# The last two down units of a two-FFN encoder layer made for 192 tokens first and then for 128, with the final norm, transposes and stores of the first part placed among the products of the second

## The reference, cut to what matters

```python
x = x + 0.5 * _swiglu(_rmsnorm(x, ffn2_norm[l]), ffn2_w_gate[l], ffn2_w_up[l], ffn2_w_down[l])
...
y = _rmsnorm(x, final_norm)

def _swiglu(x, w_gate, w_up, w_down):
    return (jax.nn.silu(x @ w_gate) * (x @ w_up)) @ w_down
```

## Time and profile before

| | |
|---|---|
| median of three runs | 2367.65 us |
| the profiled execution | 2367.89 us |
| span of its records | 2365.6 us |
| TensorE busy | 2355.6 us, 100% of the span |
| VectorE busy | 1187.0 us, 50% |
| ScalarE busy | 809.0 us, 34% |
| DMA | 347.01 MB, mean 147 GB/s |

### The profile page before, as it was taken

How to read it: one execution, slowest core, us unless ns; L and a number is a source line. 1 busy time by engine, 2 the same in 40 slices (tenths; PEclk the granted TensorE clock), 3 DMA queues, 4 the chain that set the end, 5 groups by cost and what they waited for, 6 DMA issues and landing times.

```text
span 2365.6 us, 36473 instructions
## 1 busy us (share of the span) xinstructions
PE 2355.6 (100%) x16063; PEld 2333.1 (99%) x16063; DVE 1187.0 (50%) x945; ACT 809.0 (34%) x719; POOL 123.3 (5%) x64
## 2 busy tenths in 40 slices
PE   9999999999999999999999999999999999999998
PEld 9999999999999999999999899999999999999998
DVE  5444444444444445666695456434444444443445
ACT  5323223232232324353543444233232232323324
POOL 1000000000000000100100001000000000000000
PEclk9999999999999999999999999999999999999999
DMA  7444444444444444535345134444444444444442
GB/s 251 149 148 154 142 157 144 147 155 142 156 146 148 154 143 149 189 112 178 103 139 165 55 127 160 143 151 151 143 158 142 150 151 143 158 142 152 150 143 79
DMA packets 194617, 347.01 MB, mean 147 GB/s; under 512 B 10810, under 2 KB 35904, under 8 KB 194560
## 3 DMA queue, kind: packets, MB, share of 16 engines
q1 hardware_dynamic: 190864, 337.34, 43.8%
q0 software_dynamic: 2480, 7.63, 1.0%
q10 hardware_dynamic: 1216, 1.20, 0.2%
HBM read 340.50 MB, written 5.65 MB: 146 GB/s over the span
## 4 chain that ended last, share of the span: by engine, by line
PE 99%; DVE 1%; issue 0%; ACT 0%; POOL 0%; ACTq 0%; DVEq 0%; POOLq 0%
PE ps L1613 31%; PE ps L1614 31%; PE ps L1615 31%; PE ps L2005 0%; PE ps L2025 0%; PE ps L1732 0%; PE ps L2165 0%; PE ps L1993 0%; PE ps L1728 0%; PE ps L1849 0%; PE ps L1843 0%; PE ps L1822 0%; PE ps L2006 0%; PE ps L1789 0%; PE ps L1891 0%; DVE work L1352 0%
## 5 line engine op out<-in xcount | busy, mean ns | idle before, releaser
L1613 PE MATMUL ps<-mov_hi,w_hi 128*128 128x320 f32 x3568 | 1107.1, 310 | 0.4 <-DVE w_lo L1251 0.4
L1615 PE MATMUL ps<-mov_hi,w_lo 128*128 128x320 f32 x3568 | 1102.5, 309 | 0.0
L1614 PE MATMUL ps<-mov_lo,w_hi 128*128 128x320 f32 x3568 | 1102.5, 309 | 0.0
L1043 DVE TENSOR_TENSOR w_lo<-raw,w_hi 128x2048 fp32r<-128x2048 f32 x309 | 708.2, 2292 | 740.7 <-ACT w_hi L601 740.2
L601 ACT CAST w_hi<-raw 128x2048 fp32r<-128x2048 f32 x309 | 588.5, 1905 | 1418.3 <-PE ps L1615 1418.2
L1613 PEld LDWEIGHTS ps<-mov_hi,w_hi 128*128 128x128 f32 x3568 | 669.8, 188 | 1.9 <-issue 0.7
L1614 PEld LDWEIGHTS ps<-mov_lo,w_hi 128*128 128x128 f32 x3568 | 669.8, 188 | 0.6
L1615 PEld LDWEIGHTS ps<-mov_hi,w_lo 128*128 128x128 f32 x3568 | 669.7, 188 | 0.0
L1613 PE MATMUL ps<-h_hi,w_hi 128*128 128x320 f32 x1472 | 454.7, 309 | 0.0
L1615 PE MATMUL ps<-h_hi,w_lo 128*128 128x320 f32 x1472 | 454.4, 309 | 0.0
L1614 PE MATMUL ps<-h_lo,w_hi 128*128 128x320 f32 x1472 | 454.4, 309 | 0.0
(11 more groups left out here) (257 smaller groups left out, 768.7 us busy)
## 6 DMA issues: line engine op xcount, KB each, us to landing
raw<-in_ffn_w_up SPq DMA_DIRECT2D x88, 1024.0 KB, 5.1
raw<-in_ffn_w_down SPq DMA_DIRECT2D x88, 1024.0 KB, 5.0
raw<-in_ffn_w_gate SPq DMA_DIRECT2D x87, 1024.0 KB, 5.1
raw<-in_w_in SPq DMA_DIRECT2D x28, 1024.0 KB, 5.4
raw<-in_w_out SPq DMA_DIRECT2D x16, 1024.0 KB, 5.1
raw<-in_mla_w_uq SPq DMA_DIRECT2D x12, 256.0 KB, 4.2
raw<-in_w_in SPq DMA_DIRECT2D x4, 640.0 KB, 4.3
work<-in_x_prompt SPq DMA_DIRECT2D x8, 256.0 KB, 7.7
```

Of the source, the lines that this page charges most:

```text
L1043: dve.tensor_tensor(w_lo[:, n % SPLIT_SLOTS, :], raw[:, n % RAW_SLOTS, :], w_hi[:, n % SPLIT_SLOTS, :].bitcast(F32), ALU.subtract).then_in ...
L1613: pe.matmul(out, w[0], x[0], start=first, stop=False)
L1614: pe.matmul(out, w[0], x[1], start=False, stop=False)
L1615: return pe.matmul(out, w[1], x[0], start=False, stop=last)
```

## The change

The last two down units (`q` = 2 and 3) are no longer made by `unit` for 320 tokens. A new function `part` makes a unit for a range of tokens. The order on TensorE becomes: unit 2 for tokens 128 to 319 (`EARLY`), unit 3 for the same, unit 2 for tokens 0 to 127 (`LATE`), unit 3 for those. Each part is again 48 products with 48 weight loads. The squares, folds and gains of the last two chunks are split in the same way; the token sums of the early tokens, and jobs 0, 1 and 2, are put at fixed places among the 48 products of the last part (`between`). `Y_JOBS` now has the jobs of the early token tiles first (j0 t1, j0 t2, j1 t1, j1 t2, j2 t1, j2 t2, j3 t1, j3 t2) and then the four of token tile 0. The factors are made in two steps, `spread(1, ...)` for the early tokens and `spread(2, ...)` for the late ones. The steps that ScalarE and VectorE took after `ffn` are moved into their `tail_steps`, among the drains and squares. The queues of the stores are as before (jobs 0 to 7 on SyncE, 8 to 11 on ScalarE).

```diff
-Y_JOBS = [(j, t, r0, rows) for j in range(4) for t, (r0, rows) in enumerate(TOK)]
+LATE, EARLY = slice(0, P), slice(P, T)
+Y_JOBS = [(j, t, *TOK[t]) for j in range(4) for t in (1, 2)] + [(j, 0, *TOK[0]) for j in range(4)]
...
                 def tail_steps():
+                    act.wait_ge(early_drained, 1)
+                    square_of(EARLY_SQ[0], 2, EARLY).then_inc(early_squared, 1)
+                    gain_chunk(1)
+                    act.wait_ge(early_squared, 1)
+                    gains_of(2, EARLY).then_inc(early_gained, 1)
+                    act.wait_ge(early_drained, 2)
+                    square_of(EARLY_SQ[1], 3, EARLY).then_inc(early_squared, 1)
+                    act.wait_ge(early_squared, 2)
+                    gains_of(3, EARLY).then_inc(early_gained, 1)
+                    act.wait_ge(tok_mean, 1)
+                    act.activation(tok[:, 4:6], tok[:, 1:3], ACT.Sqrt).then_inc(tok_root, 1)
+                    act.wait_ge(late_drained, 1)
+                    square_of(LATE_SQ, 2, LATE).then_inc(late_squared, 1)
+                    act.wait_ge(tok_rstd, 1)
+                    scale_even(0)
+                    act.wait_ge(late_squared, 1)
+                    gains_of(2, LATE).then_inc(late_gained, 1)
                     square_tile(0)
-                    act.wait_ge(squared, 11)
-                    gain(8)
-                    gain(9)
                     square_tile(1)
+                    scale_even(2)
                     square_tile(2)
-                    gain(10)
-                    gain(11).then_inc(y_gained, 1)
                     square_tile(3)
+                    act.wait_ge(tok_mean, 2)
+                    act.activation(tok[:, 3:4], tok[:, 0:1], ACT.Sqrt).then_inc(tok_root, 1)
+                    scale_even(4)
+                    scale_even(6)
+                    act.wait_ge(tok_rstd, 2)
+                    scale_even(8)
+                    scale_even(10)
...
+                n = T - P
+                dve.wait_ge(early_down, 1)
+                drain(2, EARLY).then_inc(early_drained, 1)
+                first_folds()
+                a, b = EARLY_SQ
+                dve.wait_ge(early_squared, 1)
+                link(fold(a, a + 2 * n, 2 * n))
+                link(fold(a, a + n, n))
+                link(fold(a, F_ACC + P, n))
+                dve.wait_ge(early_down, 2)
+                drain(3, EARLY).then_inc(early_drained, 1)
+                dve.wait_ge(early_squared, 2)
+                link(fold(b, b + 2 * n, 2 * n))
+                link(fold(b, b + n, n))
+                fold(b, a, n).then_inc(early_folded, 1)
+                dve.wait_ge(late_down, 1)
+                drain(2, LATE).then_inc(late_drained, 1)
+                mean(1, 7, 1, 3)
+                spread(1, 1, 3)
+                dve.wait_ge(late_squared, 1)
+                link(fold(LATE_SQ, LATE_SQ + 2 * P, 2 * P))
+                link(fold(LATE_SQ, LATE_SQ + P, P))
+                fold(LATE_SQ, F_ACC, P).then_inc(acc_ready, 1)
+                drain_tile(0)
+                drain_tile(1)
+                scale_odd(1)
+                gain_tile(0)
+                gain_tile(1)
+                drain_tile(2)
+                drain_tile(3)
+                scale_odd(3)
+                mean(2, 3, 0, 1)
+                gain_tile(2)
+                gain_tile(3).then_inc(y_last, 1)
+                spread(2, 0, 1)
+                for n in range(5, 12, 2):
+                    scale_odd(n)
...
+            def part(q, cols, done, tile_done=None, between=None):
+
+                n, g = U_F2 + FFN_UNITS - 4 + q, GR_F2 + FFN_GROUPS - 4 + q
+                for m in range(4):
+                    for k in range(UK):
+                        if between is not None and UK * m + k in between:
+                            between[UK * m + k]()
+                        c = UC * k + P * m
+                        w = (w_hi[:, n % SPLIT_SLOTS, c:c + P], w_lo[:, n % SPLIT_SLOTS, c:c + P])
+                        x_hi_lo = [h[:, cols] for h in hidden(k)]
+                        ins = triple(bank4(g)[:, m, cols], w, x_hi_lo, k == 0, k == UK - 1)
+                    if tile_done is not None and m < 3:
+                        ins.then_inc(tile_done, 1)
+                ins.then_inc(done, 1)
...
+            first_part(2)
+            first_part(3)
+            pe.wait_ge(early_drained, 1)
+            part(2, LATE, late_down)
+            pe.wait_ge(early_drained, 2)
+            part(3, LATE, down_tile, tile_done=down_tile,
+                 between={2: early_sums, 8: first_job, 10: lambda: y_job(1),
+                          12: lambda: pe.wait_ge(tok_mean, 1), 13: third_job})
             pe.wait_ge(y_tile, 1)
-            y_job(0)
+            y_job(3)
             pe.wait_ge(acc_ready, 1)
-            token_sums(F_ACC, P, True, False)
...
+            token_sum(3, 0, LATE_SQ, True, False)
+            for m in range(4):
+                pe.wait_ge(sq_tile, m + 1)
+                ins = token_sum(3, 0, LAST_SQ + P * m, False, m == 3)
+            ins.then_inc(tok_sum, 1)
+            pe.wait_ge(y_tile, 4)
+            for n in range(4, 12):
+                if n in (4, 6):
+                    pe.wait_ge(early_gained, n // 2 - 1)
+                if n == 10:
+                    pe.wait_ge(late_gained, 1)
+                if n == 11:
                     pe.wait_ge(y_last, 1)
                 y_job(n)
```

More of the change, by code:

```diff
@@ L718, in gain_chunk, with gains_of, square_of @@
                     last.then_inc(y_gained, 1)
-                def tail_steps():
+                def gains_of(q, cols):
+                    for j in range(4 * q, 4 * q + 4):
+                        last = act.activation(xT[:, j, cols], xT[:, j, cols], ACT.Copy,
+                                              scale=gains[:, G_FIN + j:G_FIN + j + 1])
+                    return last
+                def square_of(at, q, cols):
+                    n = cols.stop - cols.start
+                    return act.activation(wk3(at, 4, n), xT[:, 4 * q:4 * q + 4, cols], ACT.Square)
@@ new lines, in square_tile, with scale_even @@
+                def square_tile(m):
+                    act.wait_ge(y_tile, m + 1)
+                    act.activation(wk(LAST_SQ + P * m, P), xT[:, 12 + m, LATE], ACT.Square).then_inc(sq_tile, 1)
+                def scale_even(n):
+                    _, t, _, rows = Y_JOBS[n]
+                    act.wait_ge(y_turned, n + 1)
+                    act.activation(y_tokens(n), ps[0:rows, y_bank(n), :], ACT.Copy,
+                                   scale=tok[0:rows, 6 + t:7 + t]).then_inc(y_even, 1)
@@ L1015, in _ @@
             ffn(1, U_F2, GR_F2)
[L1016 to L1023, removed]
             for n in range(Y_FIRST, 12):
@@ L1201, in first_folds @@
                 dve.wait_ge(squared, 10)
-                fold(F_ACC, F_SQ, 4 * T).then_inc(sq_folded, 1)
-                dve.wait_ge(sq_folded, 1)
+                link(fold(F_ACC, F_SQ, 4 * T))
                 link(fold(F_ACC, F_ACC + 2 * T, 2 * T))
                 link(fold(F_ACC, F_ACC + T, T))
[L1207 to L1229, removed]
-                    dve.wait_ge(sq_tile, m + 1)
-                    last = dve.tensor_scalar(xT[:, 12 + m, :], xT[:, 12 + m, :], gains[:, G_FIN + 12 + m:G_FIN + 13 + m],
-                                             None, ALU.mult)
-                last.then_inc(y_last, 1)
@@ new lines, in tail_steps, with drain, drain_tile, gain_tile @@
+            def tail_steps(g):
+                def drain(q, cols):
+                    to = xT[:, 4 * q:4 * q + 4, cols]
+                    return dve.scalar_tensor_tensor(to, bank4(g + q - 2)[:, :, cols], 0.5, to, ALU.mult, ALU.add)
+                def drain_tile(m):
+                    dve.wait_ge(down_tile, m + 1)
+                    to = xT[:, 12 + m, LATE]
+                    dve.scalar_tensor_tensor(to, bank4(g + 1)[:, m, LATE], 0.5, to, ALU.mult, ALU.add).then_inc(y_tile, 1)
+                def gain_tile(m):
+                    dve.wait_ge(sq_tile, m + 1)
+                    to = xT[:, 12 + m, LATE]
+                    return dve.tensor_scalar(to, to, gains[:, G_FIN + 12 + m:G_FIN + 13 + m], None, ALU.mult)
+                def mean(e, bank, t0, t1):
+                    dve.wait_ge(tok_sum, e)
+                    dve.tensor_scalar(tok[:, t0:t1], ps[:, bank, P * t0:P * t1:P], 1.0 / D, EPS,
+                                      ALU.mult, ALU.add).then_inc(tok_mean, 1)
+                def spread(e, t0, t1):
+                    dve.wait_ge(tok_mean, e)
+                    dve.wait_ge(tok_root, e)
+                    y, a, v = tok[:, 3 + t0:3 + t1], tok[:, 6 + t0:6 + t1], tok[:, t0:t1]
+                    link(dve.reciprocal(y, y))
+                    link(dve.tensor_tensor(a, y, y, ALU.mult))
+                    link(dve.scalar_tensor_tensor(a, a, -0.5, v, ALU.mult, ALU.mult))
+                    dve.scalar_tensor_tensor(a, a, 1.5, y, ALU.add, ALU.mult).then_inc(tok_rstd, 1)
```

(19 more changed lines are left out.)

64 lines of the change are left out of this document (24 added, 40 removed).

## The result

The changed kernel takes 2371.41 us (median of 18 runs, 2370.93 to 2372.77) where the kernel before takes 2367.22 (median of 18, 2366.55 to 2367.91). The ratio is 1.0018, 95% interval 1.0012 to 1.0025: 4.2 us slower, which the interval tells from no change. The median lies just inside the 0.2% (4.7 us) that the prediction had set as its bound between "same" and "slower"; the interval reaches to both sides of it. The forecast was 2374.0 with a range from 2368.3 to 2379.0.

A forecast was written before the change was run, and what follows sets the result against it. TensorE was taken to bound the kernel, with 99% of the last-ending chain. Products +8.2, inserts +2.2 and tail -4.15 made +6.3 us on 2367.65, so 2374.0 us, range 2368.3 to 2379.0.

The forecast's parts named there:

- The cause and the sign: Last two down units: 96 more weight loads, a floor of 116 ns under each narrower product, make the kernel slower.
- Rival (a): Last two units: moving side alone sets the price, 93 and 66 ns a product, about 2367.9 us; chance 0.16.
- rival (b): Last two units: narrow fp32r products at plain fp32's pace, 2406 us, or 2379.1 with one pass; chance 0.06.
- Products: Last two units: 192 products at 116 ns, 22.3 us in place of 14.07, so 8.2 us more.
- Inserts: Among the late products: two early sums, twelve transposes and four returns to fp32r, together 2.2 us.
- Tail: From the last product to the end of the span: 12.0 us in place of 16.15, so 4.15 us less.
- The landing of the last stores: End of the tail: last stores take 4.3 us from issue to landing; named the likeliest failure after the floor.
- the likeliest case: Whole change: weight loads set a floor under the narrow products; forecast 2374.0 us, own range 2372.0 to 2376.0, chance 0.74.
- one lower bound, of the floor or of the tail: Products 0.7 us less or tail 1.3 us less; either was said to bring the time within 0.2%, chance 0.07.
- work taken out of the tail: Early sums and jobs 0 to 2 put among the late products: their 2.2 us were counted as saved behind them.
- The waits: Last units and tail: last weights, drains, folds and early factor ready in time, costed at nothing; 0.5 to 1.5 us without cover.
- Rival (c): Tail: VectorE's queue makes the late half lag, late factor at S+5 or later (S: products done), 2376 to 2378 us; chance 0.04.

The follow-up runs named there:

- two groups: Kernel before, each tile of the last two units made in two column groups in place (128 and 192 tokens), nothing else moved: 2374.43 us, 7.6 over before.
- three groups: Kernel before, last two units made in three column groups in place (128, 128 and 64 tokens): 2384.86 us, 18.0 over before.
- half weights: Kernel before with last two units cut at token 128 in place, each product made twice with 64 of 128 weight columns: 2381.48 us, 14.3 over before.
- run with the jobs behind: Changed kernel, but jobs 0, 1 and 2 transposed behind the last product, their scalings behind the last squares and drains: 2371.53 us, 4.7 over before.
- half the form: Changed kernel, but only the very last unit split by tokens, the unit before it made whole: 2367.69 us, ratio to before 1.0003.

## Why the prediction was right, and where it was off

**The cause and the sign were right.** The weight load of an fp32r product stands as a floor under it., the 188 ns of the load beside the 192 of plain fp32, and the 112.5 ns pace of the earlier trace rows told it before any fp32r product narrower than 256 was to be seen. The runs show it as a floor by itself (two groups, +7.6), in proportion to the number of loads (three groups, +18.0), and gone with half of the weight columns (half weights). Rival (a) would have needed 93 and 66 ns, rival (b) 170 or more; neither is there. Rival (a)'s formula, with a smaller constant (7 to 9 ns), fits once the weights are 64 columns wide.

**The size was too large**, 6.3 us where 4.2 came, and all three terms leaned the same way:

- Products: +8.2 by the floor of 116 ns. Measured 111.6 ns (the run with two groups), +7.35. The step that was mis-sized is the choice between 112.5 and 119: the 12 ns that an fp32r product takes over its columns at 256 and 320 don't add to the load. The lower bound, 7.5, was nearly right.
- Inserts: 2.2; measured 1.63. A group of four transposes and the return to products costs 0.37 + 0.03 us, not 0.46 + 0.085.
- Tail: -4.15; measured -4.98. The late factor at S+3.0 (said S+3.35) and the last scaling at S+6.0 (S+6.3) make 0.3 of it. The rest is the way from there to the end: 1.0 + 4.3 + 0.5 were said, 0.5 + 4.3 + 0.4 came. The landing of the last stores, named as the second weakest step, was right at 4.3; what was too large is the 1.0 us from the last scaling to the last issue.

With 7.35, 1.63 and -4.98 the sum is +4.0. The time lies within the stated range, but 0.6 below the likeliest case's own range (0.4 of that is the time before, 2367.22 in these runs and 2367.65 when the range was made), and under the 4.7 us of the bound, for which I had given "same" only 0.19. The prediction says that one lower bound, of the floor or of the tail, brings the time within 0.2%. By its own sum that is wrong: the lower bound of the floor alone leaves 5.6 us, that of the tail alone 5.0; it takes both. Here each of the three terms came out 0.6 to 0.9 us lower. The chance of 0.77 for "slower by over 0.2%" was too high for a sum that lay 1.6 us over the bound. That the time fell inside the range is owed to its width, which the rivals had given it, as much as to the sum.

**The waits.** None of those that were costed at nothing came: `w_lo` was ready (2338.77) 0.9 us before its part began, the early folds 2.5 us before the sums. Rival (c) did not occur.

**What hid what.** The text counted the inserts as "work taken out of the tail". The run with the jobs behind shows that this is a zero sum on PE. Of the 4.98 us that the tail gave back, some 1.6 are the inserts' own time, paid before S. The rest, some 3.4, I put down to the factor of the early tokens being ready in time: fewer scalings that wait for the late factor, and stores that leave before the late ones (2.3 to 3.0 us are lost when they are held back). No run takes the early factor away by itself, so this division is not shown. It stood against 7.35 us for 96 more loads, and it did not win in this form. In half the form it draws.

## What to carry to other kernels

Before a unit is cut by its moving columns, compare the pace of the weight loads with the moving side at the new width: here 64, 128 and 192 columns all cost 112 ns (an estimate from these and from the 119 ns of 256 columns puts the crossing near 240 columns), so a cut of 320 into 192 + 128 has a price per added load (77 ns), and is not a free reordering. Cut only as many units as the work to be hidden needs; one unit of 48 products gave nearly the same tail here as two (11.36 and 11.17 us). Work moved from behind the last product to among the products gains only if TensorE was not the engine that set the pace there; what did gain was data leaving before a stretch in which the DMA engines were full. How long before did not matter here: seen from the first narrow product, a first store 2.7 us later cost nothing, and one 5.4 us later cost 2.6 to 3.0 us.

## What the runs showed of the hardware beyond that

With 128x64 weights the extra time of an fp32r product over columns/2.4 GHz is 6.7 ns at 128 columns and 8.7 at 192; with 128x128 weights it was 12 to 19 at 256 to 512. The two do not differ in kind: the line through the first two, 2.7 ns and 0.448 ns a column (an estimate from 60.0 and 88.7 ns), gives 117, 146 and 232 ns at 256, 320 and 512 columns, where 119, 146.6 and 232 were measured. So nothing in these rows shows a share of the load in a product whose moving side is the longer one; the extra time grows with the moving columns. What in the engine makes it was not tried. Four transposes among products cost 0.36 to 0.38 us and 0.03 us for the return, 100 ns a transpose; sixteen in a row (the run with the jobs behind, 2356.27 to 2358.04) cost 111 ns each.
